# Two-block transformer kernel: the top-k search's threshold and hit words move into a PSUM bank, and the convolution keeps three banks

## What is computed

```python
a = u_val * jax.nn.sigmoid(u_gate)
y = lax.conv_general_dilated(a, conv_w, ..., feature_group_count=D_CONV) + conv_b   # 31 taps
y = jax.nn.silu(layernorm(y, ln_g, ln_b)) @ w_pw2

score = jnp.einsum("bth,bths->bts", w_b, jax.nn.relu(s_raw))
score = jnp.where(causal[None], score, -jnp.inf)
_, sel = lax.top_k(score, k_top)            # k_top = 256
logits = q . kv[sel] + bias ; probs = softmax ; o = probs @ kv[sel]
```

## Time and profile before

| | |
|---|---|
| median of 3 runs | 3466.71 us (3465.79 to 3471.36) |
| the profiled execution's own time | 3461.7 us |
| its span, first to last instruction | 3459.9 us |
| PE busy / DVE busy / ACT busy / POOL busy | 3064.8 / 1953.9 / 893.7 / 961.7 us |
| mean granted clock of PE | 0.94 of full speed |
| transfers | 207.16 MB, mean 60 GB/s |

### The profile page before, as it was taken

One profiled execution on the slowest core, in us unless ns is written; L12 is line 12 of the kernel. 1 busy time (PEld: TensorE's weight loads), 2 busy tenths in 40 slices (PEclk: granted clock), 3 DMA queues, 4 the chain that ended last, 5 costly groups with the idle time before them and its releaser, 6 DMA issues.

```text
span 3459.9 us, 48765 instructions
## 1 busy us (share of the span) xinstructions
PE 3064.8 (89%) x20177; PEld 1945.1 (56%) x20394; DVE 1953.9 (56%) x2977; ACT 893.7 (26%) x1544; POOL 961.7 (28%) x1046
## 2 busy tenths in 40 slices
PE   7889886988678977888699999999998899999997
PEld 7449762775338663875365465555555744444443
DVE  2586897564689996664636445365363433333334
ACT  2250022653351031653322222231221211010001
POOL 2201661002222661002232322322322223333330
PEclk9997998999799988999789999989999899999998
DMA  7222230001200330001211111111102111111101
GB/s 250 104 85 83 98 129 30 29 8 65 93 33 28 107 122 25 29 11 77 82 37 37 49 37 37 49 37 37 49 25 86 50 37 49 49 49 61 49 25 55
DMA packets 49165, 207.16 MB, mean 60 GB/s; under 512 B 4488, under 2 KB 9776, under 8 KB 32304
## 3 DMA queue, kind: packets, MB, share of 16 engines
q1 hardware_dynamic: 42288, 195.63, 16.0%
q10 hardware_dynamic: 6656, 8.39, 0.8%
HBM read 187.22 MB, written 16.79 MB: 59 GB/s over the span
## 4 chain that ended last, share of the span: by engine, by line
PE 68%; DVE 24%; issue 4%; ACT 2%; DMA 1%; POOL 1%; SPq 0%; DVEq 0%; ACTq 0%; POOLq 0%
PE big L264 15%; PE big L265 15%; PE big L263 15%; DVE arena L1525 6%; PE banks L263 4%; PE banks L264 4%; PE banks L265 4%; PE banks L948 3%; PE banks L821 2%; DVE arena L1683 2%; DVE arena L1515 2%; DVE arena L1410 1%; DVE arena L1691 1%; PE big L540 1%; PE banks L540 1%
## 5 line engine op out<-in xcount | busy, mean ns | idle before, releaser
L506 POOL CAST w_hi<-stage 128x512 bf16<-128x512 f32 x520 | 314.5, 647 | 2419.1 <-PE big L265 1742.9
L510 POOL TENSOR_TENSOR w_lo<-stage,w_hi 128x512 bf16<-128x512 f32 x520 | 652.5, 1285 | 0.0
L264 PE MATMUL big<-ht_lo,w_hi 128*128 128x512 bf16 x1381 | 527.5, 382 | 30.1 <-DVE ht_lo L1416 23.5
L265 PE MATMUL big<-ht_hi,w_lo 128*128 128x512 bf16 x1380 | 526.6, 382 | 1.4
L263 PE MATMUL big<-ht_hi,w_hi 128*128 128x512 bf16 x1359 | 518.4, 381 | 1.5
L263 PE MATMUL big<-w_hi,ht_hi 128*128 128x256 bf16 (+1 forms) x1274 | 386.1, 303 | 47.8 <-DVE ht_lo L1583 30.5
L264 PE MATMUL big<-w_lo,ht_hi 128*128 128x256 bf16 (+1 forms) x1274 | 385.9, 303 | 3.8 <-DVE ht_lo L1675 3.6
L265 PE MATMUL big<-w_hi,ht_lo 128*128 128x256 bf16 (+1 forms) x1276 | 386.1, 303 | 0.7 <-issue 0.4
L1525 DVE TENSOR_SCALAR_CACHE_REDUCE arena<-arena,smalli 128x384 bf16<-128x384 f32 (+5 forms) x384 | 337.9, 942 | 2.3
L263 PEld LDWEIGHTS big<-ht_hi,w_hi 128*128 128x128 bf16 x1408 | 140.4, 100 | 189.9 <-DVE ht_lo L1416 23.9
L265 PEld LDWEIGHTS big<-ht_hi,w_lo 128*128 128x128 bf16 x1408 | 138.7, 98 | 168.7 <-issue 4.7
(11 more groups left out here) (294 smaller groups left out, 5862.2 us busy)
## 6 DMA issues: line engine op xcount, KB each, us to landing
stage<-in_w SPq DMA_DIRECT2D x130, 1024.0 KB, 4.8
arena<-in_w_ada SPq DMA_DIRECT2D x48, 512.0 KB, 4.2
arena<-in_x SPq DMA_DIRECT2D x16, 512.0 KB, 7.1
xs<-arena SPq DMA_DIRECT2D x16, 512.0 KB, 2.6
arena<-xs SPq DMA_DIRECT2D x16, 512.0 KB, 7.9
gt<-arena ACTq DMA_DIRECT2D x16, 256.0 KB, 2.6
arena<-gt ACTq DMA_DIRECT2D x16, 256.0 KB, 2.7
out_x<-arena SPq DMA_DIRECT2D x8, 512.0 KB, 2.7
```

Source lines behind the costliest of these rows:

```text
L264: pe.matmul(out, ah, bl, start=False, stop=False)
L265: return pe.matmul(out, al, bh, start=False, stop=stop)
L506: pool.tensor_copy(w_hi[:, n % RING, c0:c1], stage[:, n % RING, c0:c1]).then_inc(s_w_hi_split, mark(s_w_hi_split, n, q))
L510: ins = pool.tensor_tensor(w_lo[:, n % RING, c0:c1], stage[:, n % RING, c0:c1], w_hi[:, n % RING, c0:c1], ALU.subtract)
```

## The change

It takes `f` and `hit` out of `smalli` and puts them into the last single PSUM bank. `cand` stays in SBUF. `hit` is now plain 1 or 0, and a predicated copy writes `cand` over `f` where it is set. After the last bit `f` is copied to SBUF (`f_end`), where the rest reads it. The bank becomes a pool of its own, "f", taken by PE for the whole search just ahead of the first `conv_in`, and let go after the copy, which counts on a new semaphore. The convolution's pool has three banks.

```diff
+        s_found = ctx.enter_context(nc.semaphore("found"))
-        pools = {"big": two[0:2], "t": one[0:2], "o": one[2:4], "c": one, "c2": two[2:4], "mlp": two}
+        pools = {"big": two[0:2], "t": one[0:2], "o": one[2:4], "c": one[0:3], "f": one[3:4], "c2": two[2:4], "mlp": two}
...
+                take(pe, "f", "search", l)
                 conv_in(l, "wg", 0, 4)
...
-                f, cand, hit = [smalli[:, 8 * i:8 * i + nb] for i in range(3)]
+                f_end, cand = [smalli[:, 8 * i:8 * i + nb] for i in range(2)]
+                f, hit = [bank[3].bitcast(I32)[:, 8 * i:8 * i + nb] for i in range(2)]
...
                     step(dve.tensor_scalar(cand, f, 1 << bit, None, ALU.bitwise_xor))
                     count(lambda j: cand[:, j:j + 1].bitcast(F32))
-                    step(dve.tensor_scalar(hit, cnt, TOPK - 0.5, float(1 << bit), ALU.is_ge, ALU.mult))
-                    step(dve.tensor_tensor(f, f, hit, ALU.bitwise_xor))
+                    step(dve.tensor_scalar(hit, cnt, TOPK - 0.5, None, ALU.is_ge))
+                    step(dve.copy_predicated(f, hit, cand))
+
+                dve.tensor_copy(f_end, f).then_inc(s_found, mark(s_found, l))
+                freed(s_found, "search", l)
+                dve.wait_ge(s_found, when(s_found, l))
+                f = f_end
```

More of the change, by code:

```diff
@@ L169, in build @@
         s_ya_lo = ctx.enter_context(nc.semaphore("ya_lo"))
-        readers = (s_act_setup, s_conv_act, s_conv_dve, s_dve_setup, s_dve_step, s_gemm, s_hf, s_hgrn_act, s_hgrn_dve, s_latent_act, s_latent_dve, s_lmax, s_ot_lo, s_pt_lo, s_qt_lo, s_read_act, s_relu, s_ya_lo, s_yr, s_weigh, s_x_sum, s_x_y, s_y_half, s_y_tok, s_ya)
+        readers = (s_act_setup, s_conv_act, s_conv_dve, s_dve_setup, s_dve_step, s_found, s_gemm, s_hf, s_hgrn_act, s_hgrn_dve, s_latent_act, s_latent_dve, s_lmax, s_ot_lo, s_pt_lo, s_qt_lo, s_read_act, s_relu, s_ya_lo, s_yr, s_weigh, s_x_sum, s_x_y, s_y_half, s_y_tok, s_ya)
         sems = {s.name: s for s in readers}
```

## The result

| | before | after |
|---|---|---|
| median of four runs each | 3467.76 us (3465.79 to 3471.36) | 3437.99 us (3437.24 to 3441.71) |
| the profiled execution's own time | 3461.7 us | 3437.24 us |
| its span | 3459.9 us | 3435.4 us |
| DVE busy | 1953.9 us | 1896.0 us |

The ratio of the times is 0.9915, 95% interval 0.9898 to 0.9932. The change gains 29.8 us in the medians and 24.5 us between the two profiled executions, where 18.6 was forecast. 3438 lies in the range of 3437 to 3461, at its lower end. The 5.3 us between the two differences come from the profiled executions: that of before stood 6.1 us under its median, that of after 0.8.

A forecast was written before the change was run, and what follows sets the result against it. PE bounds most of the chain, but DVE sets the pace in stretches, longest in the search, where small SBUF operations wait for POOL. Layer 0 -5.8, layer 1 -13.1, dearer operations +0.3: -18.6, from 3466.7 to 3448 us; range 3437 to 3461.

The forecast's parts named there:

- rival (b): In the search, PSUM words don't spare the wait for POOL and only costs remain: 3472 or 3476 us; chance 0.07.
- (c): Search operations on PSUM words cost far more than 0.17 us each; at 1 us a bit 3472 or more; chance 0.05.
- The term of +0.3 us: Small search operations dearer by 0.02 us a bit, over the twelve bits on the path: +0.3 us.
- the forecast's term: Layer 0 in all: +4.2 for the take, -10.2 at slot 30, +0.2 for the end copy, together -5.8 us.
- the steps of the layer norm: Layer 0: L1571 near 496, L1136 1.2 us after PE's end, L1575 waiting for ACT; slot 30 10.2 us sooner.
- forecast at 13.1 us: Layer 1 in all: slot 30 comes 13.3 us sooner, less 0.2 for the end copy.
- not priced: PE's half-speed clock stretches, which new and vanished gaps may move: 3.7 us either way in each layer, outside the sum.
- 5.0 forecast: Layer 1, slot 10: 5.4 us sooner less 0.4 for the transpose xt3, so conv 0 gains 5.0 us.
- 8.7 forecast: Layer 1, slot 18: by the steps of layer 0, PE gains 8.7 us.
- Rival (d): More than summed: slow clock stretches behind the removed 6.0 and 5.1 us gaps vanish too, 3440 us; chance 0.05.
- Rival (a): The wait moves: PE or ACT gives part back, or L1569 and L1571 are held; half the gain, 3457; chance 0.12.
- The gain is carried to the end: After the search, in attention and beyond, nothing is fixed in time, so the whole 18.6 us gain reaches the end.

The follow-up runs named there:

- e1: The changed kernel with f and hit back in SBUF, its take and three banks kept; 3474.66 us, ratio 1.0009 to the kernel before.
- e8: The changed kernel with hit in SBUF and the compare in its accumulator form; 3455.45 us, ratio 0.9964 to the kernel before.
- e9: The changed kernel with only f back in SBUF, hit still in PSUM; 3464.37 us, ratio 0.9998 to the kernel before.
- e5: The changed kernel again, nothing altered, on another occasion; 3430.68 us, ratio 0.9887 to the kernel before.
- e11: The changed kernel once more, nothing altered, on a further occasion; 3436.04 us, ratio 0.988 to the kernel before.
- e6: The changed kernel with the bank only marked as taken, PE not waiting for it; 3431.24 us, ratio 0.9888 to the kernel before.
- e2: The kernel before with three banks for the convolution and nothing else; 3481.01 us, ratio 1.0013 to the kernel before.
- e3: The kernel before with the plain compare and the predicated copy, all words in SBUF; 3470.04 us, ratio 0.9995 to the kernel before.
- e12: The changed kernel without the wait at the take and with conv_x one slot sooner in layer 1; 3428.31 us, ratio 0.9855 to the kernel before.
- e4: The changed kernel with only hit in SBUF, f still in PSUM; 3480.89 us, ratio 1.0005 to the kernel before.

## Why the prediction was right, and where it was not

**The mechanism** held as given: the three lines are clean at 164, 168 and 172 ns, and e1 gives the whole gain back by moving twelve words a partition into SBUF. So rival (b) is out, and (c) with it: PSUM words cost 9 ns a bit less than before, not 20 ns more. The term of +0.3 us was nothing. By the Trainium skill, "VectorE: DVE Perf Modes", section "The TRN2 errata — SBUF-src ops pay a fixed extra latency per instruction", the two PSUM readers were to cost 0.13 us a bit more, as an estimate; the trace does not agree: 164 ns for the trial from PSUM, 172 from SBUF. The rule in the Trainium skill, "SBUF — State Buffer", section "Who interferes with whom", on which DVE instructions contend with GpSimd (POOL), agrees with every run, e8's compare and e9's copy included. How long they are held is another matter (see the last section).

**The size** was too low, and the number came out right in part by luck. The forecast gain of 18.6 us stands against 29.8 here, 38.4 beside e5 and 42.6 beside e11, and the changed kernel's 3430.68 and 3436.04 us of those two lie below the range.

**Layer 0.** The take cost 4.66 - 0.44 = 4.2 us, as said. `gates_by_token(1)` was to end 0.2 us sooner, and 0.4 came in from stages in front; it ended 0.7 sooner. The slots between did not go as said: DVE's first `conv_x` started 5.7 us later (353.46, now 359.16), 1.9 more than the take and the 0.4 explain, because stretches of half speed moved (from the first `conv_in` to there the clock was granted at 0.81 before and at 0.79 now). The one at 415 to 421 us then vanished and gave it back: PE's wait for `conv_x` at slot 18 ended at 416.15 and now 416.99, its next wait for POOL at 451.54 and now 450.53. `out_half` came 6.3 sooner, 5.8 without the 0.4. That is the forecast's term, and the steps of the layer norm are the ones that made it: L1574 starts at 495.84 ("near 496"), ACT's L1138 1.0 us after PE's end, L1578 waits for ACT.

**Layer 1** was forecast at 13.1 us and gave 24.8 - 7.2 = 17.6. The two windows from the first `conv_in` to the end of `gates_by_token(1)`, of before:

```profile
1045.87:1280.20 234.33, 210.24 (x1852) 178.90 (x1856) 221.03 (x475) 26.05 (x34) 121.03 (x144) 0.93 0.26 88
```

and of after:

```profile
1038.69:1259.83 221.14, 202.42 (x1855) 173.62 (x1860) 197.51 (x490) 28.71 (x38) 121.25 (x145) 0.98 0.28 95
```

Of 13.2 us, 5.4 are idle time of PE that is gone (24.1 to 18.7) and 7.8 are PE's busy time, which fell by that much at the same number of matmuls: the clock went from 0.93 to 0.98. The step that failed is the one set aside as **not priced**, "3.7 us either way": before has five stretches of half speed here, 30.7 us in all, after two of 10.2. Up to conv 4 the sum held, place by place. From the first `conv_in`, PE began conv 0 4.7 us sooner (76.37 us after it, now 1110.32 - 1038.69 = 71.63; 5.0 forecast) and conv 4 9.3 us sooner (139.77, now 1169.13 - 1038.69 = 130.44; 8.7 forecast). Behind conv 4 the sum had nothing, and 3.9 us more came. The windows from there to the end of `gates_by_token(1)`, before and after:

```profile
1185.64:1280.20 94.56, 86.18 (x778) 67.82 (x780) 86.24 (x173) 12.38 (x17) 60.51 (x73) 0.91 0.38 129
...
1169.13:1259.83 90.70, 81.64 (x781) 64.80 (x784) 74.93 (x187) 15.42 (x22) 64.19 (x77) 0.98 0.41 137
```

PE's idle time grew there by 0.7 us and its busy time fell by 4.5 at the same number of matmuls, as the clock rose from 0.91 to 0.98. Ahead of conv 4 the clock's gain went in part into waiting: PE came to slot 10 sooner than DVE could, and its wait there grew from 5.1 to 6.3 us. So 5.4 us of idle time went, where the sum had all of its 8.7 from there. Rival (d) was this in kind. Of the two gaps it named, the 6.0 us one went, and a stretch of half speed beside it (414.7 to 421.5) with it; the 5.1 us one stayed, as did a stretch right behind it (1121.3 to 1128.1 before, 1107.1 to 1113.9 after). That a shorter gap kept the clock up is argued from these rows; no run held the clock and changed the gaps.

**Rival (a)** was there in kind as well: L1574 is held 2.8 and 3.4 us. It cost nothing, by the cover named (ACT ahead of PE's end).

**"The gain is carried to the end"** was wrong in the small: 24.8 us at `out_half` were 28.0 in the recurrent block and 24.2 at the last chunk. e5, e6 and e11 show the same in kind: e11 lost 7.0 us to e5 between `out_half` of layer 1 and the last chunk, in instructions that no edit touches.

**The waits' own size** was taken from one profile. They are not one sum. In the kernel before, a compare was issued 4.33 us into a chunk of POOL's (started 451.43), with 9.1 us of POOL's run left:

```profile
451.43 2.28 POOL L506 CAST w_hi<-stage 128x512 bf16<-128x512 f32 x4
...
455.76 0.21 DVE L1644 TENSOR_SCALAR smalli<-small 128x6 int32<-128x6 f32 x1
```

e1 has two such compares, both as far into a chunk and with as much left (the first of these runs ended at 475.29):

```profile
461.87 2.28 POOL L507 CAST w_hi<-stage 128x512 bf16<-128x512 f32 x4
...
466.20 0.21 DVE L1647 TENSOR_SCALAR smalli<-small 128x6 int32<-128x6 f32 x1
...
1225.11 2.28 POOL L507 CAST w_hi<-stage 128x512 bf16<-128x512 f32 x4
...
1229.44 9.11 DVE L1647 TENSOR_SCALAR smalli<-small 128x6 int32<-128x6 f32 x1
...
1234.03 4.49 POOL L511 TENSOR_TENSOR w_lo<-stage,w_hi 128x512 bf16<-128x512 f32 x4
```

Two passed at the next edge of a POOL instruction, the third stood until POOL's run ended (1234.03 + 4.49 = 1238.5). The phases agree to 0.01 us, and the last two are one line of one execution, so neither the phase, as far as the trace resolves it, nor the form tells them apart. What decides between 0.2 and 9 us stays open. It fits that the profiled execution of before, with only two such long holds, lay under its median; e2 and e3, which differ from it in nothing that shields DVE, show a 6.9 us hold that it lacks. Chance of this kind may also be why the kernel before spreads over 20 us and more, but that is not shown: e12, in which the three lines are clean, spreads over 16 us in six runs, three near 3434 us at a clock of 0.941 or 0.942 and three near 3421 at 0.948 or 0.949. The clock spreads the times as well.

## What to carry over

When a small operation's longest duration is many times its median, look at what the other engine on its ports does at that moment, and compare with a neighbour whose operand lies elsewhere; the sum of the excess is a first guess at the prize. Protect every operation of the loop, since what stayed exposed took back all of the gain in e4 and e9 and two thirds in e8. A few words that a loop updates may live in PSUM: at six columns that cost nothing per operation here, only a bank. Price the clock by the window's busy time at equal counts, not only by the waits that go, and read a gain at a checkpoint right behind the change as well as at the end.

## What was not expected of the hardware

- A DVE operation of six columns can wait for a whole back-to-back run of POOL's instructions, 12.2 us in before, 15.6 in e4 and 16.5 in e8. Most wait only for the one instruction that they meet: the xor of before never took more than 1.09 us. In before and e1 to e4, e8 and e9 together, 43 of the small operations took over 1.5 us, and each of them ended within 0.03 us of the end of a run of POOL's. The Trainium skill, "SBUF — State Buffer", section "Who interferes with whom", speaks of the pair being held for the whole instruction; a single subtraction of POOL's takes 1.1 us in such a run (4.49 us for four).
- The long wait can strike an operation with two SBUF inputs as well: the copy in e8, whose destination is in PSUM, waited 16.5 us. The same copy in e4, right behind an exposed compare, never took more than 1.10.
- A predicated copy with mask and destination in PSUM takes 172 ns at six columns, as one wholly in SBUF does (172 in e1).
- In three executions of one and the same kernel, the same stretch of the recurrent block took 112.5, 107.7 and 105.6 us, with the clock granted at 0.85, 0.92 and 0.97.
